# Two-layer diffusion backbone on one core: the gated rows of the feed-forward blocks split on ScalarE and VectorE, modulation pieces moved, and a weight split put between a piece's halves

## The reference

```python
def modulate(x, g, shift, scale):
    return rms_norm(x, g) * (1 + scale) + shift

def swiglu(h, w1, w2):
    a, b = jnp.split(h @ w1, 2, axis=-1)
    return (jax.nn.silu(a) * b) @ w2
...
    for layer in range(DEPTH):
        ...
        ml = jnp.split((sc @ w_mod[layer] + b_mod[layer])[:, None, :], N_MOD, axis=-1)
        ...
        h = h + 0.5 * ml[2] * swiglu(modulate(h, norm_g[layer, 0], ml[0], ml[1]), ffn_w1[layer, 0], ffn_w2[layer, 0])
        ...   # the mixer: retention and an S5 scan in layer 0, neighbourhood attention in layer 1
        h = h + 0.5 * ml[8] * swiglu(modulate(h, norm_g[layer, 2], ml[6], ml[7]), ffn_w1[layer, 1], ffn_w2[layer, 1])
    return rms_norm(h, final_g)
```

## Time and profile before

| what | us |
|---|---|
| median of 3 runs | 2156.55 (2156.18 to 2161.2) |
| the profiled execution's own time | 2155.88 |
| its span in the profile | 2154.1 |
| TensorE busy | 1892.5 (88%) |
| VectorE busy | 1306.9 (61%) |
| ScalarE busy | 653.9 (30%) |
| GpSimd busy | 443.2 (21%) |

### The profile page before, as it was taken

One profiled execution on the slowest core, in us unless ns is written; L12 is line 12 of the kernel. 1 busy time (PEld: TensorE's weight loads), 2 busy tenths in 40 slices (PEclk: granted clock), 3 DMA queues, 4 the chain that ended last, 5 costly groups with the idle time before them and its releaser, 6 DMA issues. The chain is left out here.

```text
span 2154.1 us, 26731 instructions
## 1 busy us (share of the span) xinstructions
PE 1892.5 (88%) x9708; PEld 1554.9 (72%) x9708; DVE 1306.9 (61%) x1907; ACT 653.9 (30%) x771; POOL 443.2 (21%) x415
## 2 busy tenths in 40 slices
PE   4899999978655478799999988999999799988998
PEld 1787887757544455578788766878888687678997
DVE  6887588668799735488768764345333524545544
ACT  3221122251222234333212224312222423445433
POOL 3221022120255300322102213110112200012112
PEclk8999999989877789899999999999999899999999
DMA  7344444422000111234535432233222331023553
GB/s 324 133 180 171 180 164 187 156 80 78 20 1 0 40 49 42 95 157 163 198 145 206 179 141 72 89 127 141 97 76 101 143 115 54 1 79 117 175 195 117
DMA packets 39807, 257.95 MB, mean 120 GB/s; under 512 B 4800, under 2 KB 5952, under 8 KB 14784
## 3 DMA queue, kind: packets, MB, share of 16 engines
q1 hardware_dynamic: 39744, 257.13, 32.0%
HBM read 256.06 MB, written 1.05 MB: 119 GB/s over the span
## 5 line engine op out<-in xcount | busy, mean ns | idle before, releaser
L1462 PE MATMUL ps_all<-a_lo,w_hi 128*128 128x512 f32 (+1 forms) x1808 | 669.2, 370 | 96.0 <-DVE a_lo L920 51.8
L1463 PE MATMUL ps_all<-a_hi,w_lo 128*128 128x512 f32 (+1 forms) x1808 | 663.1, 367 | 0.0
L1464 PE MATMUL ps_all<-a_hi,w_hi 128*128 128x512 f32 (+1 forms) x1808 | 662.7, 367 | 0.0
L832 DVE TENSOR_TENSOR w_lo<-w_raw,w_hi 128x2048 fp32r<-128x2048 f32 (+3 forms) x184 | 391.4, 2127 | 197.4 <-ACT w_hi L524 190.0
L1462 PEld LDWEIGHTS ps_all<-a_lo,w_hi 128*128 128x128 f32 x1808 | 348.9, 193 | 166.4 <-issue 47.6
L524 ACT ACTIVATE w_hi<-w_raw 128x2048 fp32r<-128x2048 f32 (+3 forms) x183 | 314.2, 1717 | 406.5 <-PE ps_all L1464 335.9
L1464 PEld LDWEIGHTS ps_all<-a_hi,w_hi 128*128 128x128 f32 x1808 | 348.8, 193 | 54.1
L1463 PEld LDWEIGHTS ps_all<-a_hi,w_lo 128*128 128x128 f32 x1808 | 349.4, 193 | 52.5
L842 DVE SCALAR_TENSOR_TENSOR mod_junk<-mod_raw,cond 128x1024 bf16<-128x1024 f32 x256 | 365.7, 1481 | 10.8 <-DMA mod_raw<-in_w_mod 10.6
L1462 PE MATMUL ps_all<-g_lo,w_hi 128*128 128x512 f32 (+1 forms) x704 | 259.8, 369 | 20.7 <-DVE w_lo L832 19.8
L1464 PE MATMUL ps_all<-g_hi,w_hi 128*128 128x512 f32 (+1 forms) x704 | 258.7, 367 | 0.0
(11 more groups left out here) (194 smaller groups left out, 1720.9 us busy)
## 6 DMA issues: line engine op xcount, KB each, us to landing
w_raw<-in_tiles SPq DMA_DIRECT2D x118, 1024.0 KB, 4.8
mod_raw<-in_w_mod SPq DMA_DIRECT2D x64, 1024.0 KB, 4.8
w_raw<-in_tiles SPq DMA_DIRECT2D x32, 768.0 KB, 5.2
w_raw<-in_tiles SPq DMA_DIRECT2D x32, 640.0 KB, 4.5
start_raw<-in_w_mod SPq DMA_DIRECT2D x4, 1024.0 KB, 16.4
start_scale<-in_w_scale SPq DMA_DIRECT2D x4, 1024.0 KB, 20.6
bias<-in_na_bias SPq DMA_DIRECT2D x2, 1536.0 KB, 8.4
h<-in_h SPq DMA_DIRECT2D x1, 2048.0 KB, 16.7
```

The lines of the kernel that those rows point to most:

```text
L832: nc.vector.tensor_tensor(w_lo[:, slot, 0:size], w_raw[:, slot, 0:size], w_hi[:, slot, 0:size].bitcast(F32), ALU.subtract).then_inc(lo_rea ...
L1462: pe.matmul(dst, w[0], x[1], start=start, stop=False)
L1463: pe.matmul(dst, w[1], x[0], start=False, stop=False)
L1464: return pe.matmul(dst, w[0], x[0], start=False, stop=stop_)
```

## The change

Four things are changed. The split of the gated rows leaves GpSimd: ScalarE writes g_hi right behind sil, after waiting for gated, and VectorE writes g_lo right behind gated, after waiting for g_hi. The modulation units are no longer beside ffn0.down1, ffn1.down1 and ffn2.down0 (4 units each); the 12 go beside the 12 pieces of ffn2.up0, and the numbers of the units in between shift. In a piece with a unit, VectorE now does two of the four SCALAR_TENSOR_TENSOR, then the w_lo of the next piece, then the other two and the small addition. The count that `g_split` started with is gone.

```diff
-MOD_BESIDE = {"ffn0.up0": (8, 2), "ffn0.down0": (20, 1), "ffn0.up1": (24, 2), "ffn0.down1": (34, 1),
-              "ffn1.up0": (38, 2), "ffn1.down0": (50, 1), "ffn1.up1": (54, 2), "ffn1.down1": (64, 1),
-              "ffn2.down0": (68, 1)}
+MOD_BESIDE = {"ffn0.up0": (8, 2), "ffn0.down0": (20, 1), "ffn0.up1": (24, 2),
+              "ffn1.up0": (34, 2), "ffn1.down0": (46, 1), "ffn1.up1": (50, 2),
+              "ffn2.up0": (60, 2)}
...
                         nc.scalar.activation(sil[:, slot, t0:T], ps[slot][:, 0, t0:T], ACT.Silu).then_inc(sil_ready, 1)
+                        act.wait_ge(ps_free[slot], BASE[segment] // 2 + it + 1)
+                        g = g_hi[:, bass.ds(2 * it + slot, 1), t0:T].rearrange("p a t -> p (a t)")
+                        nc.scalar.activation(g, gated[:, slot, t0:T], ACT.Copy).then_inc(g_hi_ready, 1)
...
                 for n in range(4):
                     c, v = n // 2, n % 2
+                    if between and n == 2:
+                        between()
...
-                        mod_beside(segment, it, slot)
-                        split_lo(n + 1, nxt, 1 - slot)
+                        mod_beside(segment, it, slot, lambda: split_lo(n + 1, nxt, 1 - slot))
                         dve.wait_ge(sil_ready, g_base(segment) + 2 * it + slot + 1)
-
-                        dve.wait_ge(g_split, g_base(segment) + 2 * it + slot + 1)
                         nc.vector.tensor_tensor(gated[:, slot, t0:T], sil[:, slot, t0:T], ps[slot][:, 1, t0:T],
                                                 ALU.mult).then_inc(ps_free[slot], 1)
+                        j = 2 * it + slot
+                        dve.wait_ge(g_hi_ready, g_base(segment) + j + 1)
+                        hi, lo = [x[:, bass.ds(j, 1), t0:T].rearrange("p a t -> p (a t)") for x in (g_hi, g_lo)]
+                        nc.vector.tensor_tensor(lo, gated[:, slot, t0:T], hi.bitcast(F32),
+                                                ALU.subtract).then_inc(g_split, 1)
...
-            def up(segment):
-
-                t0 = FFN_T0[int(segment[3])]
-                with pool.Fori(0, SIZE[segment] // 2) as it:
...
-                        nc.gpsimd.tensor_copy(hi, gated[:, slot, t0:T]).then_inc(pool_hi, 1)
-                        pool.wait_ge(pool_hi, g_base(segment) + j + 1)
-                        nc.gpsimd.tensor_tensor(lo, gated[:, slot, t0:T], hi.bitcast(F32),
-                                                ALU.subtract).then_inc(g_split, 1)
```

More of the change, by code:

```diff
@@ L313, in program @@
         normed_ready, a_ready, gain_ready = sem("normed_ready"), sem("a_ready"), sem("gain_ready")
-        pool_hi = sem("pool_hi")
+        g_hi_ready = sem("g_hi_ready")
         dve_chain = sem("dve_chain")
@@ L833, in split_lo, with mod_unit @@
                                         w_hi[:, slot, 0:size].bitcast(F32), ALU.subtract).then_inc(lo_ready, 1)
-            def mod_unit(u, raw, junk, acc):
+            def mod_unit(u, raw, junk, acc, between=None):
                 done = 4 * u if early(u, FIRST_UNITS // 2) else 4 * (u - FIRST_UNITS // 2)
@@ L848, in mod_unit, with mod_beside @@
                                         ALU.add).then_inc(mod_ready, 1)
-            def mod_beside(segment, it, slot):
+            def mod_beside(segment, it, slot, split):
                 first, per = MOD_BESIDE.get(segment, (0, 0))
@@ L854, in mod_beside @@
                     dve.wait_ge(mod_in[slot], 16 * (MOD_LOADS[segment][slot] + it + 1))
-                    mod_unit(first + per * it + slot, mod_raw[:, slot], mod_junk, slot)
+                    mod_unit(first + per * it + slot, mod_raw[:, slot], mod_junk, slot, split)
+                else:
+                    split()
             def up(segment):
@@ L898, in body, with split @@
                         n = BASE[segment] + 2 * it + slot
[L899 to L903, removed]
+                        def split():
+                            if not (last and slot):
+                                split_lo(n + 1, width(segment), 1 - slot)
+                            elif nxt:
+                                split_lo(n + 1, width(nxt), 1 - slot)
+                        mod_beside(segment, it, slot, split)
                         residual(n, slot, 2 * it + slot, 1, FFN_T0[f])
@@ L1372, in norm @@
                                             ALU.mult).then_inc(scaled_ready, 1)
-            def up(segment):
-                t0 = FFN_T0[int(segment[3])]
-                with pool.Fori(0, SIZE[segment] // 2) as it:
-                    for slot in range(2):
-                        j = 2 * it + slot
-                        pool.wait_ge(ps_free[slot], BASE[segment] // 2 + it + 1)
-                        hi = g_hi[:, bass.ds(j, 1), t0:T].rearrange("p a t -> p (a t)")
-                        lo = g_lo[:, bass.ds(j, 1), t0:T].rearrange("p a t -> p (a t)")
-                        nc.gpsimd.tensor_copy(hi, gated[:, slot, t0:T]).then_inc(pool_hi, 1)
-                        pool.wait_ge(pool_hi, g_base(segment) + j + 1)
-                        nc.gpsimd.tensor_tensor(lo, gated[:, slot, t0:T], hi.bitcast(F32),
-                                                ALU.subtract).then_inc(g_split, 1)
             def mixer0():
@@ L1440, in mixer1 @@
                 norm(4)
-            nc.gpsimd.memset(half_pi[:], float(np.pi / 2)).then_inc(g_split, 2)
+            nc.gpsimd.memset(half_pi[:], float(np.pi / 2))
             for f in range(4):
@@ L1449, in _ @@
                 norm(NORM_OF[f])
-                for b in range(2):
-                    up(f"ffn{f}.up{b}")
             add_squares(6)
@@ L1490, in down @@
                 t0, K = FFN_T0[f], BLOCKS[b]
-                g_end = 2 + g_base(segment) + K
+                g_end = g_base(segment) + K
                 with pe.Fori(0, SIZE[segment] // 2) as it:
```

## The result

| | before | after |
|---|---|---|
| median, us | 2157.23 (2156.18 to 2161.2, 4 runs) | 2193.18 (2191.91 to 2194.43, 4 runs) |
| ratio to before | | 1.0162 [1.0149, 1.0175] |
| span of the profiled execution | 2154.1 | 2190.0 |

The change makes the kernel 36 us slower.

The account below looks back on a forecast made before the run. TensorE, busy for 88% of the span, was taken as the bound, so only its waits count. 45.8 + 3.2 - 14.8 - 3.6 = +30.6 us took the profiled 2155.88 to 2186.5, the median to 2187; range 2158 to 2213.

Parts of the forecast that it names:

- the first case: The prediction's own sum of all terms: 2187 us, range 2174 to 2202, chance 0.70.
- The gain in the down segments: Waits for w_lo vanish where units leave: -14.8 us in ffn0.down1 and ffn1.down1 together, -3.6 in ffn2.down0.
- The ring: Unit segments: odd weight tile, w_hi, w_lo and unit's end wait in a circle, 23.7 us against TensorE's 21.76 per pass.
- The table load: ffn1.up0 and ffn2.up0: ScalarE's load ahead of w_hi, behind the tile's landing, lengthens the circle of waits to 25.06 us.
- ffn1.up0 with down0: From ffn1.up0's start to piece 1 of down0, w_lo comes later: 1065.2 against 1053.37, +11.8 us.
- up1 of ffn0 and ffn1: No table load; the first pass has just room enough, three wait 1.94 each: +11.6 us for both segments.
- ffn2.up0: Newly given units: ten pieces take 123.9 us instead of 108.8, plus 0.2 at the start: +15.3 us.
- ffn3: Without units: g_hi delays the table load 0.89 us, up0 pays +3.6, up1 +0; sum +3.2.
- g_hi is dear: Rival: each VectorE, ScalarE, VectorE hand-over costs 0.6 us more, so ffn3's up1 waits too: 2214 us, chance 0.10.
- The sign that I had set for it: Sign of "g_hi is dear": g_hi starts over 0.1 us behind gated's end, or takes over 0.8.
- The first rival: The odd weight tile lands 1.9 us sooner, TensorE keeps its pace in all five unit segments: 2136 us, chance 0.13.
- Half of it: Rival: the circle of waits in unit segments is 22.7 us, so its waits halve: 2163 us at the top, chance 0.07.

Follow-up runs that it names:

- only_moved: The kernel before with only the units' table changed: none beside ffn0.down1, ffn1.down1, ffn2.down0, twelve beside ffn2.up0; 2144.6 us, ratio 0.9945.
- weights_first: The changed kernel with both weight tiles of a pass issued ahead of both unit transfers on SyncE; 2132.99 us, ratio 0.9884.
- early_unit: The changed kernel with SyncE's wait for slot 0's unit transfer loosened by one unit, order of issues kept; 2134.05 us, ratio 0.9887.
- whole_unit: The changed kernel with all four parts of a unit together again on VectorE, ahead of w_lo; 2148.54 us, ratio 0.9951.
- only_halves: The kernel before with only the next piece's w_lo put between the two halves of a unit; 2177.6 us, ratio 1.0092.

## Why the prediction was right

2193.18 lies 6 above the forecast of 2187 and inside the first case's own range; between the profiled executions it was +30.6 forecast and +35.9 measured. Point by point:

- **The gain in the down segments.** Forecast 14.8 and 3.6, measured 16.8 and 3.5. The waits of the two down1 are gone in full, and 1.0 more in each: a wait costs TensorE some 0.25 more than its row says, because the pieces otherwise overlap by 0.16 and the first products behind a wait are slower by 0.08. I had priced the waits by their rows. only_moved shows the same three numbers.
- **The ring.** Forecast 23.7, measured 23.83 to 23.91 in ffn0.up0 behind the first. Two runs that open it in different places (weights_first, early_unit) and one that takes VectorE's order back (whole_unit) make every wait in these passes go, and only_halves has it alone. The mis-sized term is the hand-over from gated over g_hi to g_lo. I had ScalarE and VectorE start 0.03 behind each other; g_hi starts 140.32 - 140.20 = 0.12 behind gated's end and g_lo 0.16 behind g_hi's: the way from gated's end to g_lo's start is 0.91, and I had 0.68. g_hi itself takes 0.63, as the square did. The longer hand-over stands only in the hardware loops. In the pass written out behind the loop it is 0.03 and 0.03, as I had it: there gated ends at 187.68 in ffn0.up0, and ScalarE's g_hi and VectorE's g_lo are

```profile
187.71 0.63 ACT L539 ACTIVATE g_hi<-gated 128x512 fp32r<-128x512 f32 x1 [4.16 <-DVE gated L873]
...
188.37 0.69 DVE L878 TENSOR_TENSOR g_lo<-gated,g_hi 128x512 fp32r<-128x512 f32 x1 [0.70 <-ACT g_hi L539]
```

  In the loop g_hi and g_lo are addressed by the loop's count; that this makes the difference is likely, and no run tried it.
- **The table load.** Forecast 25.06 for the ring, measured 25.10 to 25.12; the run without the loads has 23.89. Six of the eight rings lie between 25.10 and 25.24; the first of each segment was longer, 25.61 in ffn1.up0 and 26.64 in ffn2.up0 (the latter below).
- **ffn1.up0 with down0.** Forecast +11.8, measured +12.3; ffn0 +7.1 and +6.8. Both are closer than their terms, by luck: the rings up to piece 11 are 1.6 and 1.2 us longer together than I had, and the step from there to piece 1 of down0 takes 22.0 and 21.6, where I had 23.2. down0's smaller weight tile lands sooner (w_hi starts 202.37 - 196.21 = 6.16 behind the issue) and its first w_lo is shorter too; I had counted only the shorter w_hi.
- **up1 of ffn0 and ffn1.** Forecast +5.8 each, measured +6.7 and +8.9. In ffn0 the three rings are 0.2 longer each than I had, and the first has 0.3 too little room. In ffn1 it is 2.2 more than in ffn0, most of it from two places. The last ring is 24.64 long (1233.76 - 1209.12): its weight tile is issued at 1224.26 and w_hi starts at 1231.81, 7.55 later. And the last piece takes 12.5 us, where ffn0's takes 11.2, behind a wait of 2.54 and at a granted clock of 0.88; no later wait takes that up. I had put the clock at 0, with 5 at worst.
- **ffn2.up0.** Forecast +15.3, measured +17.5. The first ring is 26.64 long, not 25.06. VectorE in it:

```profile
1350.92 1.22 DVE L847 SCALAR_TENSOR_TENSOR mod_junk<-mod_raw,cond 128x1024 bf16<-128x1024 f32 x1 [4.15 <-DMA mod_raw<-in_w_mod]
...
1356.71 2.29 DVE L835 TENSOR_TENSOR w_lo<-w_raw,w_hi 128x2048 fp32r<-128x2048 f32 x1 [3.41 <-ACT w_hi L524]
```

SyncE ahead of it:

```profile
1344.67 0.33 SPq L460 DMA_DIRECT2D mod_raw<-in_w_mod  x1
1345.19 0.33 SPq L468 DMA_DIRECT2D w_raw<-in_tiles  x1
1345.72 0.33 SPq L460 DMA_DIRECT2D mod_raw<-in_w_mod  x1
1346.59 0.33 SPq L468 DMA_DIRECT2D w_raw<-in_tiles  x1
```

The unit's data is there 6.25 behind its issue, against 125.85 - 121.08 = 4.77 in the earlier trace rows. That four transfers go out within 2 us is not the reason, for they do so in the passes of usual length too: in the next one from 1371.31 to 1373.24, and VectorE has the unit's data 4.80 behind its issue there (1376.11). This ring has something else beside it, a packet on a queue that loads instructions. The DMA view from 1344.5 to 1351 has the line

```profile
q8 instruction: 1, 0.02, 0.9%
```

and the same view from 1371.2 to 1377.5 has none. Over the whole of after, a weight tile issued right behind a unit's transfer lands 6.1 to 7.0 us behind its own issue in 29 cases and 7.1 to 8.2 in five, and an instruction packet falls into each of the five and into none of the 29. The five are just the rings that came out long: the first of ffn0.up0 (24.19), of ffn1.up0 (25.61) and of ffn2.up0 (26.64), and the last of ffn1.up0 and ffn1.up1 (24.61 and 24.64). The match isn't perfect in the other kernels: in before one tile takes 7.1 without such a packet. No run moved the loading of instructions, so the cause is argued and not shown.

- **ffn3.** Forecast +3.2, measured +4.9. In up0 the table load comes later, as forecast: TensorE's waits at pieces 3, 5, 7 and 9 grow by 1.0 each, from 0.28 to 1.28, where I had 0.89. The first pieces of down0 and down1 cost 0.55 and 0.5, where I had 0.5 for both; the 0.9 of the wait for g_lo went as forecast. ScalarE in after, which answers to the earlier trace rows:

```profile
1992.67 0.38 ACT L536 ACTIVATE sil<-ps_all 128x256 f32<-128x256 f32 x1 [4.88 <-PE ps_all L1458]
1993.65 0.42 ACT L539 ACTIVATE g_hi<-gated 128x256 f32 x1 [0.60 <-DVE gated L873]
1994.09 1.28 ACT L524 ACT_TABLE_LOAD   x1
1995.38 1.91 ACT L524 ACTIVATE w_hi<-w_raw 128x2048 fp32r<-128x2048 f32 x1
```

From sil's end to the load it is 1.04 us, and before the load followed sil at once. The 0.91 of room in up1, which I said 0.89 just fills, is overdrawn a little: +0.8 over the segment. The rival "g_hi is dear" had found the right weak place, but with 0.6 too much a hand-over; it was 0.2. The sign that I had set for it came by the letter: g_hi starts 0.12 behind gated's end, over the 0.1 that I named. So that sign was set too near to tell this rival from my sum; its other half, a g_hi over 0.8, did not come (0.63).

The first rival (the tile lands in time) fell: the tile takes 6.82 from its issue. "Half of it" fell with the ring's 23.9. What I named as signs of being right came as said: parts at 1.22, g_lo at 0.69, no waits in down1. One of the signs did not come whole: the waits in ffn1.up0 aren't equal but between 1.4 and 3.1, since behind a slow piece the next ring is already further on.

## What to carry to other kernels

When an instruction is moved ahead of the one that frees a buffer, follow the free-signal through the issuing queue before counting what the move wins: here a count of `mod_ready` held a weight tile that had nothing to do with it, merely because it stood behind in the same queue. A loop whose way round is longer than the bound engine's pace costs the difference in each pass, however idle all engines are; add it up from row to row and compare it with the pace. And order what a queue issues by who needs it first: that one line took 60 us off the changed kernel.

## What the runs showed of the hardware

- **The clock behind waits.** Pieces behind some waits ran at a granted clock between the two levels of 1.2 and 2.4 GHz. Stretches of after, a piece each (us, busy us by engine, clock, DMA share, GB/s): piece 5 of ffn1.up0 behind a wait of 3.06 us, and piece 7 behind one of 1.43:

```profile
975.20:988.00 12.80, 12.75 (x49) 10.39 (x50) 10.71 (x17) 2.44 (x2) 0.00 (x0) 0.87 0.00 0
...
1000.30:1011.50 11.20, 11.15 (x49) 9.26 (x50) 10.03 (x15) 2.44 (x2) 0.00 (x0) 1.00 0.00 0
```

  The first is 1.6 us longer. But piece 9, behind a wait of 3.06 too, kept the full clock (1.00 from 1025.5 to 1036.5), and piece 5 of ffn1.up1 fell behind 1.86 (0.86 from 1187.6 to 1200.1). So the length of the wait before a piece doesn't decide it alone; what does is open. Within a chain of rings it costs nothing, since the next wait is shorter by as much (3.06, then 1.43); at a segment's last piece it counts.
- **Hand-overs.** From gated on VectorE to g_hi on ScalarE 0.12 us and from there to g_lo 0.16 in the loop over ffn0.up0, but 0.03 each in the pass written out behind it, as from w_hi to w_lo.
- **VectorE beside GpSimd.** A w_lo of the same shape took 3.37 beside GpSimd's split and 2.29 without it (only_halves, above). The Trainium skill, page "SBUF — State Buffer", section "Who interferes with whom", says that a VectorE instruction with two SBUF inputs contends with a GpSimd instruction that reads SBUF; the trace agrees. It is 1.08 us of VectorE's time, and the ring is no longer for it than in after (23.84 and 23.91), because there the hand-overs of the gated rows take as much.
